# Scaling the next step's probabilities before the row maximum two steps on, with the value products one step later

## The reference, cut to what matters

```python
def _mha(q, k, v):
    s = jnp.einsum('bhqd,bhkd->bhqk', q, k).astype(jnp.float32) * HEAD_DIM ** -0.5
    p = jax.nn.softmax(s, axis=-1).astype(v.dtype)
    return jnp.einsum('bhqk,bhkd->bhqd', p, v)

def merge_branches(u, ys):
    acc = jax.nn.sigmoid(proj(u, 'gate0')) * (ys[0] @ w_branch[0])
    for i in range(1, N_BRANCH):
        acc = acc + jax.nn.sigmoid(proj(u, 'gate%d' % i)) * (ys[i] @ w_branch[i])
    return acc @ w_out
```

## Time and profile before

| | us |
|---|---|
| median of three runs | 2534.37 (2529.94 to 2536.66) |
| the profiled execution | 2532.3 |
| its span | 2530.5 |
| TensorE busy | 2428.9 (96%) |
| VectorE busy | 1581.3 (62%) |
| ScalarE busy | 1064.8 (42%) |
| GpSimd busy | 27.4 (1%) |
| DMA, mean over the span | 131 GB/s |

### The profile page before, as it was taken

The page is one execution under the profiler, slowest core; times in us unless marked ns, Lnnn a source line. Parts: engine busy times, 40 slices in busy tenths (PEclk is TensorE's granted clock), DMA queues, the critical chain, the costliest instruction groups (busy, mean ns, idle before and its releaser), DMA issues.

```text
span 2530.5 us, 31850 instructions
## 1 busy us (share of the span) xinstructions
PE 2428.9 (96%) x12584; PEld 1973.4 (78%) x12584; DVE 1581.3 (62%) x2620; ACT 1064.8 (42%) x1842; POOL 27.4 (1%) x43
## 2 busy tenths in 40 slices
PE   6999998999999999989999989999989999988998
PEld 3888886877767676768888868888868788778998
DVE  2798888355455557688887874333355456588654
ACT  5222235355454535462222342222354555556444
POOL 0000000000000000000000000000000000000000
PEclk9999999999999999999999999999999999999999
DMA  5556554321322112225655523322234243233554
GB/s 234 184 207 216 187 178 159 95 76 63 104 71 71 63 67 84 71 88 192 210 206 191 186 99 108 100 99 85 96 113 141 76 142 121 88 125 126 185 178 154
DMA packets 98069, 331.42 MB, mean 131 GB/s; under 512 B 11009, under 2 KB 12033, under 8 KB 97281
## 3 DMA queue, kind: packets, MB, share of 16 engines
q1 hardware_dynamic: 97922, 329.39, 38.4%
HBM read 323.06 MB, written 6.29 MB: 130 GB/s over the span
## 4 chain that ended last, share of the span: by engine, by line
PE 90%; DVE 4%; ACT 3%; issue 1%; DMA 1%; SPq 0%; POOL 0%; DVEq 0%; ACTq 0%
PE ps L347 26%; PE ps L338 24%; PE ps L339 24%; PE ps L649 5%; PE ps L1180 3%; PE ps L1155 3%; PE ps L1165 3%; DVE w_low L327 1%; ACT w_high L321 1%; ACT prob L1304 0%; PE ps L548 0%; DMA mod_first<-in_mods 0%; DVE stat L1464 0%; PE ps L1124 0%; ACT pt L1314 0%
## 5 line engine op out<-in xcount | busy, mean ns | idle before, releaser
L327 DVE TENSOR_TENSOR w_low<-raw,w_high 128x1024 fp32r<-128x1024 f32 (+1 forms) x488 | 551.7, 1136 | 495.3 <-ACT w_high L321 494.5
L321 ACT ACTIVATE w_high<-raw 128x1024 fp32r<-128x1024 f32 (+1 forms) x488 | 481.6, 990 | 762.1 <-DMA raw<-in_weights 761.9
L338 PE MATMUL ps<-u_high,w_high 128*128 128x512 f32 (+1 forms) x2208 | 771.0, 361 | 4.2 <-DVE acc L1421 1.4
L339 PE MATMUL ps<-u_low,w_high 128*128 128x512 f32 (+1 forms) x2208 | 762.6, 357 | 0.0
L347 PE MATMUL ps<-u_high,w_low 128*128 128x512 f32 (+1 forms) x2496 | 542.9, 362 | 4.8 <-DVE w_low L327 4.8
L347 PEld LDWEIGHTS ps<-u_high,w_low 128*128 128x128 f32 x2496 | 422.5, 190 | 91.6 <-issue 19.7
L338 PEld LDWEIGHTS ps<-u_high,w_high 128*128 128x128 f32 x2208 | 418.8, 190 | 89.4 <-issue 17.1
L339 PEld LDWEIGHTS ps<-u_low,w_high 128*128 128x128 f32 x2208 | 418.9, 190 | 58.1
L410 DVE CUSTOM_DVE_ANT_0 ps<-mod_raw,c_all,smalls 128x1024 f32<-128x1024 f32 x256 | 319.5, 1290 | 2.2 <-DMA mod_raw<-in_mods 1.7
L338 PE MATMUL ps<-hid_high,w_high 128*128 128x512 f32 (+1 forms) x704 | 249.0, 362 | 0.0
L339 PE MATMUL ps<-hid_low,w_high 128*128 128x512 f32 (+1 forms) x704 | 249.0, 362 | 0.0
(11 more groups left out here) (151 smaller groups left out, 2258.5 us busy)
## 6 DMA issues: line engine op xcount, KB each, us to landing
raw<-in_weights SPq DMA_DIRECT2D x360, 512.0 KB, 3.5
mod_raw<-in_mods SPq DMA_DIRECT2D x128, 512.0 KB, 4.2
raw<-in_weights SPq DMA_DIRECT2D x64, 384.0 KB, 3.1
raw<-in_weights SPq DMA_DIRECT2D x64, 320.0 KB, 2.9
mod_first<-in_mods SPq DMA_DIRECT2D x16, 512.0 KB, 13.1
h_kept<-h SPq DMA_DIRECT2D x16, 256.0 KB, 2.0
na_bias<-in_na_rows SPq DMA_DIRECT2D x16, 256.0 KB, 4.0
h<-h_kept SPq DMA_DIRECT2D x2, 2048.0 KB, 8.0
```

Source lines behind the costliest of these rows:

```text
L321: act.activation(w_high[s][:, 0:width], raw[s][:, 0:width], ACT.Copy).then_inc(high_made.sem, 1)
L327: dve.tensor_tensor(w_low[s][:, 0:width], raw[s][:, 0:width], w_high[s][:, 0:width], ALU.subtract).then_inc(low_made.sem, 1)
L338: pe.matmul(o, w_high[s][:, w], x_high(x), start=first and a == 0, stop=False)
L339: pe.matmul(o, w_high[s][:, w], x_low(x), start=False, stop=False)
```

## The change

In branches B, C and D VectorE runs `scale_probs(j + 1)` before `row_max(j + 2)`, with the first point's splits ahead of both. `mix(p)`, with `high_of_out(p)` and `low_of_out(p)`, is done in step 2p + 3 instead of 2p + 2, for all p but the last. Branch A keeps both orders.

```diff
@@ TensorE's loop
-                    if j % 2 == 0 and j:
-                        mix(j // 2 - 1)
+                    for p in self.mixes(j):
+                        mix(p)
                     flip(j)
@@ ScalarE's loop
                     keep_probs(j)
-                    if j % 2 == 0 and j:
-                        high_of_out(j // 2 - 1)
+                    for p in self.mixes(j):
+                        high_of_out(p)
@@
+            def mixes(self, j):
+
+                after = 2 if self.b == "A" else 3
+                return [p for p in range(self.NP - 1) if 2 * p + after == j]
@@ VectorE's loop
                 scale_probs(0)
                 for j in range(J):
-                    if j + self.early < J:
-                        row_max(j + self.early)
+                    if not self.deep and j + 1 < J:
+                        row_max(j + 1)
                     self.window_splits(dve, split_low, 1 + 2 * j)
                     if j + 1 < J:
                         scale_probs(j + 1)
+                    if self.deep and j + 2 < J:
+                        row_max(j + 2)
                     if b == "A":
@@
-                    elif j % 2 == 0 and j:
-                        low_of_out(j // 2 - 1)
+                    else:
+                        for p in self.mixes(j):
+                            low_of_out(p)
                     self.window_splits(dve, split_low, 2 + 2 * j)
```

## The result

| | before | after |
|---|---|---|
| median of five runs, us | 2536.07 | 2551.09 (2549.26 to 2562.79) |
| ratio, 95% interval | 1 | 1.0084 (1.0069 to 1.0098) |
| the profiled execution, us | 2532.3 | 2562.8 |
| first FLIP to last MIX, D0 | 67.22 | 76.28 |
| the same, D1 | 35.64 | 42.18 |

The change makes the kernel slower, by 15 us between the medians and by 0.84% (21 us, 17 to 25) in the ratio. 2549.7 was forecast. The profiled execution after happens to be the slowest of its five, and part of its 30 us goes with the granted clock (0.981 against 0.988 over the whole span); so the loops are read from it, and the size of the whole from the ratio. The ratio is larger than the quotient of the two medians (1.0059), and the executions of the changed kernel lie far apart: 2549.3, 2550.5, 2551.1, 2557.5 and 2562.8 us.

A forecast was written before the change was run, and what follows sets the result against it. TensorE, busy for 96% of the span, was taken as the bound. 6.8 (D1) + 6.0 (D0) + 1.4 (ends) + 0.5 (C1) + 1.6 (clock) - 1.0 (gain) = 15.3 us on 2534.4 gave 2549.7, range 2538 to 2559.

The forecast's parts named there:

- The chain: Deep branches: row maximum waits behind scaling, scaling for exponentials, next exponentials for that maximum; 5.02 us a turn, 7.06 with early split.
- D0, 6.0 us: Branch D's layer-0 softmax loop, 16 steps of 512 or 256 keys: 6.0 us longer, turn of 4.85 against step of 4.39.
- D1, 6.8 us: Branch D's layer-1 softmax loop, 8 steps of 512 keys: 6.8 us longer, 5.9 of it by the last FLIP.
- The ends of B0 and C0, 1.4 us: Layer-0 loops of branches B and C: last MIX waits 0.72 us more for its neighbour's halves, 1.4 us in all.
- B1, C1: Layer-1 loops of branches B and C: chain hidden, nothing for B; C tight, 0.5 us for one gate evacuation.
- The gain of 1.0 us: FLIPs or gate products coming a little early in a few steps: 1.0 us off, between 0 and 3.
- Rival 2: Faster: early scaling removes 0.3 to 0.4 us waits at FLIP and gate products, chain hidden; -4 us, 2530; chance 0.08.
- The clock, 1.6 us: TensorE's granted clock falls after one of two new long waits in branch D: 1.6 us, between 0 and 3.4.
- rival 3: Worse: each longer wait drops the clock, 3.4 us, and lags add 2 to 3 in each D; 2556 to 2560; chance 0.10.
- Rival 1: Slack holds in branch D's uneven steps, only ends and start-up show: about +4 us, 2538; chance 0.20.

The follow-up runs named there:

- second profile: The changed kernel run once more, unaltered, on another chip, against the kernel before: ratio 1.0084 (1.0072 to 1.0097).
- The second row maximum: Branch D's row maximum taken twice, the extra result unused: ratio 1.0052 in the kernel before, 1.0188 in the changed kernel, both against the kernel before.

## Why the prediction was right, and where it was off

- **The chain.** Right in mechanism and size. The turn of 5.02 us measured 5.03, the one with a split 7.04 for 7.06; `exps(5)` of D0 was to start 1.98 us later than before, and with the loop's own start 3.8 us later it did (992.84 for 992.85). The order alone brings it out and D left alone takes it away. The kernel with the splits behind the maximum shows the 2.04 us of a split by taking it out.
- **D0, 6.0 us.** Right. The order alone makes the loop 5.2 longer, and the last MIX stands 0.9 further behind it: 6.1. The changed kernel's loop is 8.2 longer (8.1 in its second profile); the other 3.0 are the first stretch at the lower clock.
- **D1, 6.8 us.** Right in sum: 6.5 and 6.6 in the two profiles. Its parts were partly others than followed. In the loop 5.9 was forecast; the order alone gives 4.1 (4.7 at an equal clock), and about 1.5 come from `mix(2)`, which stands behind the last wait for the gate's bank and was not in the working. The end gives 0.9. At full clock the two waits for that bank are 2.05 and 1.94 us, where 2.9 and 1.0 were forecast.
- **The ends of B0 and C0, 1.4 us.** Mis-sized. They are 1.6 each, 3.2 together. The last MIX waits 0.88 longer, not 0.72, and 0.7 came from a place that was not looked at: the deferred MIX had covered the evacuation between two window products.
- **B1, C1.** The loops hid the chain, as said; 0.15 and 0.16 us, for 0 and 0.5.
- **The gain of 1.0 us.** Not found as a gain of the early scaling. D0's 1.3 with the products alone is 1.0 for one product past one wait, and B0's loss is the same thing the other way round. Rival 2 falls with B0: the order alone scales early there, the chain is hidden, and the loop is 88.45 us for 88.44. The kernel that scales ahead of the splits without the chain is no faster than its base either.
- **The clock, 1.6 us.** Mis-sized, and the widest miss: 5.5 us in both profiles, beyond the 0 to 3.4 stated. A drop behind `scores(7)`'s wait was foreseen, but it cost 2.95 and not 1.6. The second, 2.55 us behind D0's last MIX, was not looked for. The drop that was feared at D1's wait for the gate came in one profile of two and cost nothing: the loop is 39.15 us with it and 39.16 without, since the next wait for the bank was shorter by as much (0.47 for 1.94).
- **The sum.** 8.2 (D0's loop with its drop) + 2.55 (the drop behind it) + 5.7 (D1's loop) + 4 x 0.9 (last MIX in B0, C0, D0, D1) + 1.4 (the loops of B0 and C0) + 0.3 (B1, C1), about 21.7, where 15.3 was forecast and the ratio says 21 (17 to 25). Without the two drops it is 16.2. The stages behind D0 are longer by 4.7 us in both profiles; the 2.1 us beside the drop were not followed, and are no more than those stages differ between the other kernels without a drop there (915.5 to 917.8 us). The two halves alone give 0.52% + 0.23% = 0.75%, which the intervals don't tell from 0.84%.
- **Luck.** That the median of 2551.09 lies only 1.4 us from 2549.7 is partly chance. Three of the five executions are of the faster group, and the sum of 15.3 fits those; by the ratio the change costs 21 us, which on 2534.4 is 2556, in rival 3's place. Rival 3's mechanism, more than one drop of the clock, is what both profiles show, though without its 2 to 3 us more in each D. (Its own terms reach 2557.5, not the 2560 it gives.)
- **Rival 1**, the slack in D, was wrong: idle VectorE time in D0 was inside the chain. The second row maximum shows it, for the idle time takes most of the extra work in the order of before and hardly any in the new one.

The kernel before with the first scaling ahead of the first splits is the version to keep: 0.29% faster than before (0.18 to 0.39), one swapped pair of calls.

## What to carry to other kernels

In a loop that is pipelined two steps deep over in-order queues, write down for each instruction what it waits for, and then what stands behind it: moving an instruction ahead of one that was ready makes the second wait for everything that the first waits for, and the turn of that ring, set against the length of a step, says whether it costs. A step with little matrix work to hide it is the place to compute this for, not the average one. When a product is deferred, look at what it was covering and at the last one, whose neighbour in the bank moves closer.

## What was not expected of the hardware

A wait of TensorE of 1.9 us cost more than itself. With the wait before D0's first FLIP cut to 0.17 us, the granted clock stayed at 1.00 through the loop, where it had been 0.52 (mostly 1.2 GHz instead of 2.4) over the next 3.5 us, and the loop became 1.5 us shorter. In the changed kernel the 2.63 us wait for `exps(5)` was followed by a stretch at 0.58 over 7.35 us in one profile, and at 0.59 in the other.

But equal waits don't have equal results. At D1's high product of window 6 the changed kernel waited 2.04 us in its first profile and 2.05 in its second; over the next 3 us the granted clock was 0.50 in the first and 1.00 in the second:

```profile
2291.06:2294.06 3.00, 3.00 (x14) 3.00 (x15) 2.86 (x8) 2.08 (x3) 0.00 (x0) 0.50 0.00 0
```

```profile
2287.19:2290.19 3.00, 3.00 (x25) 3.00 (x26) 2.86 (x8) 2.08 (x3) 0.00 (x0) 1.00 0.00 0
```

With VectorE's order alone the wait there was 2.81 us, and the clock stayed at 1.00. So the clock is a cost of waits that doesn't come each time, and it counts only where the work behind the wait sets the pace. No run here holds the clock fixed.
